# The first slices by quarters, loads in the order of use, and fill products in a hybrid decoder step

## The reference, cut to what matters

```python
mod = jax.nn.silu(c.astype(jnp.float32)) @ ada_w + ada_b
shift, scale, gate = jnp.split(mod, 3, axis=-1)
h = rmsnorm(x, g_pre) * (1.0 + scale[:, None]) + shift[:, None]
z = h @ w_in
...
gates = jax.nn.sigmoid(h @ w_merge + b_merge)
g_a, g_b = jnp.split(gates, 2, axis=-1)
out = rmsnorm((g_a * ya + g_b * yb) @ w_out, g_post)
y = x.astype(jnp.float32) + gate[:, None] * out
```

## Time and profile before

| what | value |
|---|---|
| median of 3 runs | 933.63 us (932.96 to 933.76) |
| profiled execution | 933.39 us, span 931.6 us |
| tensor engine busy | 905.5 us (97%) |
| VectorE busy | 556.0 us (60%) |
| ScalarE busy | 418.0 us (45%) |
| DMA, one queue | 233.72 MB, 68.0% of 16 engines' span |
| mean granted clock | 0.995 |

### The profile page before, as it was taken

One profiled execution on the slowest core, in us unless ns is written; L12 is line 12 of the kernel. 1 busy time (PEld: TensorE's weight loads), 2 busy tenths in 40 slices (PEclk: granted clock), 3 DMA queues, 4 the chain that ended last, 5 costly groups with the idle time before them and its releaser, 6 DMA issues.

```text
span 931.6 us, 18640 instructions
## 1 busy us (share of the span) xinstructions
PE 905.5 (97%) x7762; PEld 868.6 (93%) x7762; DVE 556.0 (60%) x808; ACT 418.0 (45%) x514; POOL 54.9 (6%) x38
## 2 busy tenths in 40 slices
PE   3899999999999999999999999999999999999997
PEld 1788989999999999999999999999999999999997
DVE  4777776476675767757576655336454444445554
ACT  4323227455565565646554434444344333343330
POOL 0000000001101010110102122000000000000000
PEclk9899999999999999999999999999999999999999
DMA  9999975848585684857675565476687666645535
GB/s 373 418 421 419 419 311 171 332 158 284 183 323 197 226 301 158 314 179 293 231 268 187 199 203 183 154 271 189 254 323 281 257 243 255 246 161 181 182 136 186
DMA packets 43322, 234.57 MB, mean 252 GB/s; under 512 B 9088, under 2 KB 14592, under 8 KB 16256
## 3 DMA queue, kind: packets, MB, share of 16 engines
q1 hardware_dynamic: 43264, 233.72, 68.0%
HBM read 219.33 MB, written 14.38 MB: 251 GB/s over the span
## 4 chain that ended last, share of the span: by engine, by line
PE 94%; DVE 2%; DMA 2%; issue 1%; POOL 1%; ACT 0%; SPq 0%; DVEq 0%; POOLq 0%; ACTq 0%
PE bank L429 25%; PE bank L430 24%; PE bank L431 24%; PE bank L481 4%; PE bank L482 3%; PE bank L483 3%; PE bank L403 3%; PE bank L413 1%; DMA raw<-stream 1%; PE bank L577 1%; PE bank L622 1%; PE bank L561 1%; DMA sel<-sel_in 1%; DVE raw L1429 1%; DVE w_lo L1028 0%
## 5 line engine op out<-in xcount | busy, mean ns | idle before, releaser
L429 PE MATMUL bank<-h_hi,w_hi 128*128 128x264 f32 x1280 | 368.2, 288 | 2.2 <-DVE w_lo L1028 1.3
L430 PE MATMUL bank<-h_lo,w_hi 128*128 128x264 f32 x1280 | 362.9, 283 | 0.0
L431 PE MATMUL bank<-h_hi,w_lo 128*128 128x264 f32 x1280 | 362.5, 283 | 0.0
L1028 DVE TENSOR_TENSOR w_lo<-raw,w_hi 128x2048 fp32r<-128x2048 f32 x119 | 272.3, 2288 | 142.1 <-PE bank L431 142.0
L712 ACT ACTIVATE w_hi<-raw 128x2048 fp32r<-128x2048 f32 x120 | 229.7, 1914 | 44.0 <-DMA raw<-stream 23.8
L429 PEld LDWEIGHTS bank<-h_hi,w_hi 128*128 128x128 f32 x1280 | 241.1, 188 | 8.5 <-issue 6.4
L430 PEld LDWEIGHTS bank<-h_lo,w_hi 128*128 128x128 f32 x1280 | 241.3, 189 | 0.3
L431 PEld LDWEIGHTS bank<-h_hi,w_lo 128*128 128x128 f32 x1280 | 240.1, 188 | 0.0
L481 PE MATMUL bank<-h_hi,w_hi 128*128 128x264 f32 x256 | 76.1, 297 | 4.5 <-DVE h_lo L1110 4.5
L482 PE MATMUL bank<-h_lo,w_hi 128*128 128x264 f32 x256 | 73.7, 288 | 0.0
L483 PE MATMUL bank<-h_hi,w_lo 128*128 128x264 f32 x256 | 73.6, 288 | 0.0
(11 more groups left out here) (180 smaller groups left out, 1181.4 us busy)
## 6 DMA issues: line engine op xcount, KB each, us to landing
raw<-stream SPq DMA_DIRECT2D x120, 1024.0 KB, 5.0
ada_ring<-ada SPq DMA_DIRECT2D x32, 1024.0 KB, 15.5
raw<-first_w SPq DMA_DIRECT2D x16, 1024.0 KB, 13.1
gate_ring<-ada SPq DMA_DIRECT2D x16, 1024.0 KB, 6.6
s_t<-sret SPq DMA_DIRECT2D x8, 1024.0 KB, 5.0
v_all<-v_dram SPq DMA_DIRECT2D x8, 1024.0 KB, 7.4
nret_s<-s_t SPq DMA_DIRECT2D x8, 1024.0 KB, 8.1
x_t<-xT SPq DMA_DIRECT2D x1, 2112.0 KB, 7.7
```

The source lines that it names most:

```text
L429: pe.matmul(out, wh[:, cols], hi[:, k, :], start=(k == 0), stop=False)
L430: pe.matmul(out, wh[:, cols], lo[:, k, :], start=False, stop=False)
L431: mm = pe.matmul(out, wl[:, cols], hi[:, k, :], start=False, stop=(k == depth - 1))
L1028: dve.tensor_tensor(lo, raw[:, c % 3, :], hi.bitcast(f32), ALU.subtract).then_inc(lo_ready, 1)
```

## The change

It does these things. SP loads x in four pieces; ScalarE issues the four constant loads; slice 1 and all later slices move one place back in SP's order, behind two more slot loads. The product for the mean of squares goes between slots 0 and 1 instead of 1 and 2. Fill products (`keep_busy`: identity by identity, 128 columns, into a bank that nobody reads) stand behind the slots of group 0 (3, 3, 3, 2) and behind its select (6). Slices 0 and 1 are rounded by quarters, and slices 0 to 4 are multiplied by quarters of two units each, own units first, each waiting for its quarter of `w_lo`. Group 1's slots are cut in two by the first quarter of slice 1, and select of group 1 comes after its second quarter. `h_lo` of group 0 is made after the first quarter of `w_lo`. VectorE's takes and splits are in another order in all slices. In the merge the two gate loads go behind two tiles, one each.

```diff
+BY_QUARTER, HIGH_BY_QUARTER = 5, 2
...
-            sp.dma_start(x_t[:, :, :], xT).then_inc(x_in, 16)
-            sp.dma_start(c_in[:, :, :], cT).then_inc(const_in, 16)
-            sp.dma_start(vecs[:, :], vec).then_inc(const_in, 16)
-            sp.dma_start(ident[:, :], ident_in).then_inc(const_in, 16)
-            sp.dma_start(sel[:, :], sel_in).then_inc(const_in, 16)
-            for p in range(8):
-                if p == 0:
-                    load_ada(p, range(4))
-                    load_slice(0)
-                else:
-                    load_ada(p, (0, 1))
-                    load_slice(2 * p)
-                    load_ada(p, (2, 3))
-                load_slice(2 * p + 1)
+            for n in range(4):
+                sp.dma_start(x_t[:, 4 * n:4 * n + 4, :], xT[:, 4 * n:4 * n + 4, :]).then_inc(x_in[n], 16)
+            load_ada(0, range(4))
+            load_slice(0)
+            for p in range(1, 8):
+                load_ada(p, (0, 1))
+                load_slice(2 * p - 1)
+                load_ada(p, (2, 3))
+                load_slice(2 * p)
+            load_slice(15)
...
-                if q - 1 in COND_VISITS:
-                    v = COND_VISITS.index(q - 1) + 1
-                    if v < 8:
-                        load_cond(v)
+                for s in range(2):
+                    if q - 1 - s in COND_VISITS[:7]:
+                        load_cond(COND_VISITS.index(q - 1 - s) + 1, s)
...
+            def keep_busy(times):
+
+                for _ in range(times):
+                    pe.matmul(ST[:, 0:128], ident[:, :], ident[:, :], start=True, stop=True)
+
...
-                    if u == 2:
+                    if u == 1:
...
+                    if p == 0:
+                        keep_busy(3 if s < 3 else 2)
...
+            def quarter(j, n):
+
+                if n == 0:
+                    pe.wait_ge(h_lo_ready, j // 2 + 1)
+                if n < 3:
+                    pe.wait_ge(lo_quarter, 3 * j + n + 1)
+                else:
+                    pe.wait_ge(lo_ready, j + 1)
+                for u in (2 * n, 2 * n + 1):
+                    if u < OWN_IN[j % 2]:
+                        own(j, u)
+                    else:
+                        pass_through(j, u - OWN_IN[j % 2])
...
-            for p in range(7):
-                even_slice(2 * p)
+            keep_busy(6)
+            for n in range(4):
+                quarter(0, n)
+            ada_phase(1, (0, 1))
+            quarter(1, 0)
+            ada_phase(1, (2, 3))
+            quarter(1, 1)
+            select(1)
+            quarter(1, 2)
+            quarter(1, 3)
+            for p in range(1, 7):
+                if 2 * p < BY_QUARTER:
+                    for n in range(4):
+                        quarter(2 * p, n)
+                else:
+                    even_slice(2 * p)
                 ada_phase(p + 1)
-                odd_slice(2 * p + 1, between=p + 1)
+                if 2 * p + 1 < BY_QUARTER:
+                    quarter(2 * p + 1, 0)
+                    select(p + 1)
+                    for n in range(1, 4):
+                        quarter(2 * p + 1, n)
+                else:
+                    odd_slice(2 * p + 1, between=p + 1)
...
+            split_slice(0, 0)
+            low_h(0)
+            for n in range(1, 4):
+                split_slice(0, n)
             for n in range(4):
-                split_slice(0, n)
-            low_h(0)
-            for p in range(1, 8):
+                take_sum(0, n)
+                split_slice(1, n)
+            take_sum(0, 4)
...
+            for b in range(3):
+                take_sum(14, b)
             split_slice(15, 0)
-            take_sum(14, 0)
             split_slice(15, 1)
-            take_sum(14, 1)
-            take_sum(14, 2)
+            take_sum(14, 3)
             split_slice(15, 2)
-            take_sum(14, 3)
+            take_sum(14, 4)
             split_slice(15, 3)
-            take_sum(14, 4)
-            take_sum(15, 0)
-            split(0, 0, parts=(0,))
-            take_sum(15, 1)
-            take_sum(15, 2)
-            split(0, 0, parts=(1,))
-            take_sum(15, 3)
+            for n in range(4):
+                take_sum(15, n)
+                split(0, 0, parts=(n,))
             take_sum(15, 4)
-            split(0, 0, parts=(2, 3))
             take_sum(15, 5)
```

More of the change, by code:

```diff
@@ L190, in build @@
         const_in = sem("const_in")
-        x_in = sem("x_in")
+        x_in = [sem(f"x_in{n}") for n in range(4)]
+        hi_quarter, lo_quarter = sem("hi_quarter"), sem("lo_quarter")
         trig_in = sem("trig_in")
@@ L463, in _, with ada_phase @@
             pe.wait_ge(const_ready, 1)
-            def ada_phase(p):
-                if p >= 1:
+            def keep_busy(times):
+                for _ in range(times):
+                    pe.matmul(ST[:, 0:128], ident[:, :], ident[:, :], start=True, stop=True)
+            def ada_phase(p, slots=range(4)):
+                if p >= 1 and 0 in slots:
                     pe.wait_ge(mod_ready, p)
-                for s in range(4):
+                for s in slots:
                     u = 4 * p + s
-                    if u == 2:
+                    if u == 1:
                         pe.wait_ge(x_sum, KT // 2)
@@ L495, in pass_through @@
                 n = through(j, b)
-                if b == 0:
+                if b == 0 and j >= BY_QUARTER:
                     pe.wait_ge(lo_ready, j + 1)
@@ L719, in split_slice, with split_quarter @@
                 act.activation(w_hi[:, slot, :], raw[:, slot, :], ACT.Copy).then_inc(hi_ready, 1)
+            def split_quarter(j, n):
+                slot, cols = (j + 2) % 3, slice(512 * n, 512 * n + 512)
+                if n == 0:
+                    act.wait_ge(raw_loaded[slot], 16)
+                high = act.activation(w_hi[:, slot, cols], raw[:, slot, cols], ACT.Copy)
+                if n < 3:
+                    high.then_inc(hi_quarter, 1)
+                else:
+                    high.then_inc(hi_ready, 1)
+            act.dma_start(c_in[:, :, :], cT).then_inc(const_in, 16)
+            act.dma_start(vecs[:, :], vec).then_inc(const_in, 16)
+            act.dma_start(ident[:, :], ident_in).then_inc(const_in, 16)
+            act.dma_start(sel[:, :], sel_in).then_inc(const_in, 16)
             act.wait_ge(const_in, 64)
@@ L755, in _ @@
             ada_copy(0)
-            split_slice(0)
+            split_quarter(0, 0)
             split_h(0)
-            split_slice(1)
-            for p in range(1, 8):
+            for n in range(1, 4):
+                split_quarter(0, n)
+            for n in range(4):
+                split_quarter(1, n)
+            for p in range(1, 3):
+                ada_copy(p)
+                split_slice(2 * p)
+                split_h(p)
+                split_slice(2 * p + 1)
+            for p in range(3, 8):
                 split_slice(2 * p)
@@ L1037, in split_slice @@
                 slot = (j + 2) % 3
[L1038 removed]
+                if j < HIGH_BY_QUARTER and n < 3:
+                    dve.wait_ge(hi_quarter, 3 * j + n + 1)
+                elif j < HIGH_BY_QUARTER or n == 0:
                     dve.wait_ge(hi_ready, j + 1)
[L1040 to L1041 removed]
+                if n == 0 and j >= 2:
+                    dve.wait_ge(slice_sums, sliced(j - 2))
                 cols = slice(512 * n, 512 * n + 512)
@@ L1114, in _ @@
             make_h(0)
+            split_slice(0, 0)
+            low_h(0)
+            for n in range(1, 4):
+                split_slice(0, n)
             for n in range(4):
-                split_slice(0, n)
-            low_h(0)
-            for p in range(1, 8):
+                take_sum(0, n)
+                split_slice(1, n)
+            take_sum(0, 4)
+            for p in range(1, 3):
+                if p == 2:
+                    for b in range(3):
+                        take_sum(2, b)
+                    split_slice(3, 0)
+                    split_slice(3, 1)
+                    take_sum(2, 3)
+                    split_slice(3, 2)
+                    take_sum(2, 4)
+                    split_slice(3, 3)
+                normalize(p)
+                take_sum(2 * p - 1, 0)
+                make_h(p)
+                take_sum(2 * p - 1, 1)
+                split_slice(2 * p, 0)
+                take_sum(2 * p - 1, 2)
+                low_h(p)
+                take_sum(2 * p - 1, 3)
+                split_slice(2 * p, 1)
+                take_sum(2 * p - 1, 4)
+                take_sum(2 * p - 1, 5)
+                split_slice(2 * p, 2)
+                split_slice(2 * p, 3)
+            for p in range(3, 8):
+                for b in range(3):
+                    take_sum(2 * p - 2, b)
                 split_slice(2 * p - 1, 0)
-                take_sum(2 * p - 2, 0)
                 split_slice(2 * p - 1, 1)
-                take_sum(2 * p - 2, 1)
-                take_sum(2 * p - 2, 2)
+                take_sum(2 * p - 2, 3)
```

(3 more changed lines are left out.)

22 lines of the change are left out of this document (12 added, 10 removed).

## The result

The changed kernel takes 936.19 us (median of 10 runs, 935.17 to 936.69) where the kernel before, beside it, takes 933.61. The ratio is 1.0027, 95% interval 1.0018 to 1.0036: 2.6 us slower. The profiled execution has a span of 934.5 us against 931.6, 2.9 more.

What follows compares the result with a forecast made beforehand. Tensor engine bound, busy 905.5 of 931.6 us, so only idle and low-clock time can be won. First phase 0.1 and merge 1.3 gave -1.4: 932.0, or 932.2 from the median, taken as 932.3; range 929.5 to 935.6.

Steps and rivals of the forecast that it cites:

- the 0.66: Tensor engine gap of 0.66 us at 16.76, before the product with ones; forecast to be removed.
- my latest 26.4: Start of slice 0 if the clock rises only after slot 1; 23.8 if by slot 1.
- forecast 35.8: Start of slots 6 and 7, after quarter 0 of slice 1; they were to end at 37.7.
- The anchor on the load of slice 1: Slice 1 lands at 29.0, its take ends at 30.8; tensor engine waits up to 2.5 us, earlier gains gone.
- Rival D: Slower through a low clock in the slots and slice 0: 935.5, 934.3, or 937.5 with both; chance 16%.
- The second of the two mechanisms: Rival D's clock fall in the wait inside slice 0: 20 matmuls at 0.22 cost 2.0 us, giving 934.3.
- my own chain: From slice 1 landing at 29.0 through splits, take, two units, slots 4 and 5 and quarter 0 to 35.8.
- its wait 1.1 and 0.65: Tensor engine waits after the selects of slices 1 and 3, for sums behind make_h: 1.1 and 0.65 us.
- The end of the phase: Wait of 1.2 us before slice 15, 1.05 saved before the next tile; net cost 0.15.
- The merge: First conditioning visit: one gate load moves a tile later, removing the tensor engine's 1.29 us wait; gain 1.3.
- the price: Time of one fill product: 0.57 us at half rate, 0.29 at full rate.
- forecast 67.05: Start of the modulation phase after slice 4, against 67.31 before; lead left 0.25 us.

Runs made afterwards that it cites:

- three mends: Changed kernel with constants on SyncE, product with ones between slots 1 and 2, takes and tail mended, fills kept: 933.19 us, 0.9994.
- no fills: Changed kernel with constants on SyncE, product with ones between slots 1 and 2, and `keep_busy` taken out: 934.34 us, 1.0012.
- the last run: Kernel before with merge, x pieces, slices 0 and 2 and first whole tile by quarters, new load and take order, no fills: 930.13 us, 0.9963.
- four mends: Changed kernel with constants on SyncE, product with ones later, two takes before make_h, slice 14 takes between splits, no fills: 932.55 us, 0.9989.

## Why the prediction was wrong

The forecast was 932.3 and the median is 936.19, 3.9 above it and above the range.

**The step that failed first** is "Quartered x loads, and constants issued by ScalarE, bring the sum of squares forward and remove the 0.66". They put it back by 1.6 us, from 16.76 to 18.38, and the 0.66 became 2.71. Slice 0 started at 29.85, after my latest 26.4. Three things were missed. ScalarE's squares stand behind the constants, so a sooner x cannot help them. And a small load on a second queue is not served at once: it shares each DMA engine with the big loads of the first. I had weighed the Trainium skill, DMA: Bandwidth & Descriptors, section "Issuing engines are not separate DMA queues", for bandwidth only, where it holds (the first 1 MB load is done at 12.0 in the changed kernel, at 11.8 with the constants on SyncE); that to interleave also means to be late was not drawn from it. The Trainium skill, DMA: Bandwidth & Descriptors, section "Queues, rings and completion order", says that a DMA engine takes turns between its queues a packet at a time. The run with constants on ScalarE alone agrees with turns: one small load was done per 2.5 to 2.8 us, and a small load has as many packets as a large one, 144. The third thing is the larger: the place of the product with ones was taken as neutral, and the sum has its 1.2 us but no wait before it. Ahead of slot 1 it waits for the sum of squares with three slots behind it. That alone is 4.3 us of slice 0's start with the constants late (29.85, 25.55), and 3.9 with them on SyncE (29.16; 25.24 in the run with three mends). With both put back, slice 0 started at 25.24 with fills and at 24.36 and 25.64 without, inside the 23.8 to 26.4. (The sum for 26.4 has a slip of 0.1: its terms give 22.7, not 22.6.)

This step carries all of the 4.1 us by which slot 6 is late (39.88, forecast 35.8). From the first product of slice 0 to slot 6 the changed kernel takes 10.03 us and waits for no load; the three other runs that start slice 0 late, at 29.16, 30.17 and 30.39, take 10.02 or 10.03, whether slice 1 landed at 30.7, 30.4 or 29.2.

**The anchor on the load of slice 1** did not act in the changed kernel: slice 0 ran later than the load, and the wait that I had forecast there, ended by a take near 30.8, is missing. The mechanism is right where slice 0 starts early: with the product later the wait is 2.04, with three mends 2.47, with no fills 1.45, each ended by a take. I had slice 1 land at 29.0, as the eighth load does today. The changed kernel's row for its issue at 6.54 is

```profile
DMA to landing us min/median/max: 24.2/24.2/24.2
```

which makes 30.7. Some 0.4 is the later start (first load done at 12.0 instead of 11.6). The rest is a single longer gap: loads are done every 2.5 us, but once early in each of the fourteen profiles the gap is 3.4 to 4.0, and all later loads stay late. Whether it falls before or behind slice 1 differs between executions: slice 1 landed at 30.7 here and at 29.2 in the run with the end of the phase as before, which has the same instructions up to there. In each profile that gap overlaps the first packet of the instruction queue. In the changed kernel (28 to 29 us), then in the kernel before (30 to 31 us), by queue: packets, MB, share of 16 engines:

```profile
q8 instruction: 1, 0.02, 6.7%
```

```profile
q8 instruction: 1, 0.02, 6.3%
```

6.7% of 16 engines for 1 us is 1.07 us of one engine. Loads are done at 27.0 and 30.7 around it in the changed kernel, at 31.6 and 35.0 in the kernel before. In the run with the product later the packet is at 24 to 25 and the long gap 24.3 to 27.9; in the last run at 28 to 29, and 29.1 to 32.7. But the packet alone does not explain it. The changed kernel's next one (43 to 44 us) is as long,

```profile
q8 instruction: 1, 0.02, 6.8%
```

and the loads around it are done at 43.2, 45.7 and 48.2, 2.5 apart; so are those around the two after it, at 58.0 and 74.3. In other runs some later packets do stand beside a longer gap (2.8 to 3.1 us in several, 5.1 once). What makes the difference was not tried and stays open.

**Rival D**, the clock, was on the range's edge. Its 29.8 us for the start of slice 0 and its 935.5 are close to the 29.85 and 936.19 measured, and this is chance: it had slots and fills at the lower clock throughout, while slots 2 and 3 took 1.08 and 1.07 us, and the delay is the product's place and the constants'. From slice 0 on the clock did not fall in the changed kernel: its waits of 1.34 and 0.88 left it at 1.00. The second of the two mechanisms that I gave it, a fall in the wait inside slice 0, is what the profiles show when slice 0 starts early with fills: 1.1 to 1.4 us in slots 4 and 5 and in a few matmuls.

**What the forecast would have missed even with its start.** Either single mend gives 0.7 us at slot 6 (39.18, 39.16), and both together without fills 1.9 (37.95). That is still 2.15 behind the 35.8. By my own chain 1.8 of it is the landing in that run (30.8 instead of 29.0) and 0.35 the way from there to slot 6, 7.15 us where I had 6.8. That is an estimate which no run shows: in the run with four mends slice 1 landed at 29.3 and slot 6 began at 38.16, with no wait on a sum, but slice 0 started at 25.64 and 26 of its matmuls were 0.22 apart. An early start at the higher clock with slice 1 landed by 29.3 has no profile. Nor was the new order of loads tried alone.

**From slot 6 on** the forecast held. I had 5.6 us from slots 6 and 7 to the product that waits (35.8 to 41.4), and it was 5.64; its wait 1.1 and 0.65, measured 0.88 and 0.46; 17.05 from the slots of group 2 to those of group 3, measured 17.36. My claim that these waits would come from takes behind `make_h` is shown by the releasers, and only in part by the run that moved the takes: the stretch from group 1's slots to group 3's became 0.6 us shorter where 1.3 to 2 were expected, since the waits went to the two next products, and the time did not change (1.0026, 1.0027).

**The end of the phase** held: 1.2 lost, 1.05 saved, net 0.15, against 1.12, 0.91 and 0.2. In part by chance: the 7.2 behind the 1.2 is more than the named steps add up to (3.0, three takes of 0.43 and four splits of 0.65 are 6.9, so 0.9). **The merge** held: 1.3 against 1.3 in the trace and 1.4 alone. **The fills**: the price held (0.53 for one at the lower clock, 1.58 for three from 13.82 to 15.40, and 0.29 at the higher, 0.87 from 18.75 to 19.62, in the run with fills alone; I had 0.57 and 0.29). But in neither pair of runs did the fills buy time.

**The sum**: 4.1 at slot 6 and 0.5 in the periods behind it make 4.6 at the slots of group 3 (71.65, forecast 67.05). The forecast span was 931.6 - 1.4 = 930.2; with 4.6 it is 934.8, and 934.5 was measured. All of the miss lies before 71.65 us, and nine tenths of it in the start.

## What to carry to other kernels

A load order is also an order of landing per queue: small loads that much work waits for belong in the first queue right behind the first big one (all there at 9.3 us here), not on another engine's queue beside a stream of big loads (16.9 us); ahead of the first big one was not tried. In an engine's fixed order, an instruction that waits holds up all behind it: one product moved ahead of slot 1, before its input was there, put off slice 0 by 3.9 to 4.3 us. Before moving work forward, look for the last thing that comes late in that stretch (here the load of slice 1 and the take behind its split) and for what a wait does to the clock: a head start of 3.6 us that ended there was worth 0.02 us at slot 6. And the waits on a sum are gone in the run whose order takes the sums before the split that waits for a load. That run, with another order of loads, no fills and the product at its old place as well, was 3.5 us faster than before instead of 2.6 slower.

## What the runs showed of the hardware

- Small loads on the second issuing queue were done one per large load of the first: 8.8, 11.6, 14.3 and 16.9 us beside x in one piece, last at 10.8 beside x in four pieces, at 9.3 on the same queue as x. A small load and a 1 MB load have 144 packets each.
- One instruction packet (0.02 MB) took 1.0 to 1.1 us of one DMA engine. In fourteen profiles the first one (at 23.2 to 37.4 us) stands beside a load that is done 0.9 to 1.5 us late, with all later ones; the changed kernel's next three stand beside gaps of 2.5 us, no longer than any other.
- In profiles, waits of the tensor engine of 2.04, 2.47, 2.77 and 3.78 us were followed by a granted clock of 0.5 (1.2 GHz); waits of 0.88, 1.34 and 1.45 were not.
- In the kernel before the granted clock reads 1.00 up to 21.6 us while a slot takes 1.94 us (two take 3.64 at 17.94); later, at 1.00, a slot takes 1.07. There the distance of the matmuls tells the rate, the clock's row does not. And it rose at different times in runs with the same instructions up to there: slots 2 and 3 took 3.45 us (at 18.29, four mends) and 1.07 each (at 17.81 and 19.40, no fills), which alone moved slice 0 from 24.36 to 25.64. One profile of this start is good to about 1.3 us.
